# Layer 1's q and k projected as rows with the heads' rotary parts in one block, and layer 3's input transposed in the slab ahead of it

## What is computed

```python
c_q, c_kv, k_pe, z = split(x @ w_in)                  # 512, 512, 64, 2048 columns
q  = (rms_norm(c_q, q_norm) @ w_uq).reshape(B, S, 16, 128 + 64)
q_nope, q_pe = q[..., :128], apply_rope(q[..., 128:], cos, sin)
k_pe = apply_rope(k_pe[:, :, None, :], cos, sin)[:, :, 0]      # shared by all heads
kv = (rms_norm(c_kv, kv_norm) @ w_ukv).reshape(B, S, 16, 128 + 128)
k_nope, v = kv[..., :128], kv[..., 128:]
s = (q_nope . k_nope + q_pe . k_pe) * 192 ** -0.5     # causal softmax, then times v
y = o * silu(z);  x = layer_norm(x * alpha + y @ w_out)
# layer 3 begins with
proj = rmsnorm(x, norm_g) @ w_in
```

## Time and profile before

| | |
|---|---|
| median of 3 runs | 2526.69 us (2524.89 to 2526.69) |
| the profiled execution | 2524.33 us, of which span 2522.6 us |
| TensorE busy (matmuls) | 2470.3 us, 98% |
| VectorE, ScalarE busy | 1382.7 us (55%), 1233.0 us (49%) |
| the transfers' share of 16 engines | 50.3% (weights), mean 164 GB/s |
| granted TensorE clock, mean | 0.991 |

### The profile page before, as it was taken

One profiled execution on the slowest core, in us unless ns is written; L12 is line 12 of the kernel. 1 busy time (PEld: TensorE's weight loads), 2 busy tenths in 40 slices (PEclk: granted clock), 3 DMA queues, 4 the chain that ended last, 5 costly groups with the idle time before them and its releaser, 6 DMA issues.

```text
span 2522.6 us, 30023 instructions
## 1 busy us (share of the span) xinstructions
PE 2470.3 (98%) x12030; PEld 2060.6 (82%) x12030; DVE 1382.7 (55%) x1848; ACT 1233.0 (49%) x1661; POOL 125.0 (5%) x125
## 2 busy tenths in 40 slices
PE   8999999999999999989999989999999999999999
PEld 6888888888888888868888868888888887888887
DVE  5645454645464646554545565555445466746554
ACT  4454444444454445344555345555444368645443
POOL 1101010101010101000000000000000000000000
PEclk9999999999999999989999989999999999999999
DMA  7545555555555554635533545555555555433344
GB/s 239 188 159 185 166 184 167 181 164 173 171 172 175 183 167 151 217 125 187 180 117 116 186 143 177 174 184 173 182 173 164 179 184 161 137 103 117 101 134 134
DMA packets 342048, 414.49 MB, mean 164 GB/s; under 512 B 19019, under 2 KB 269093, under 8 KB 341397
## 3 DMA queue, kind: packets, MB, share of 16 engines
q1 hardware_dynamic: 340500, 405.63, 50.3%
q0 software_dynamic: 1408, 6.94, 0.7%
HBM read 410.42 MB, written 2.10 MB: 164 GB/s over the span
## 4 chain that ended last, share of the span: by engine, by line
PE 92%; DVE 3%; ACT 3%; issue 1%; SPq 0%; DMA 0%; POOL 0%; DVEq 0%; ACTq 0%
PE ps L557 26%; PE ps L559 26%; PE ps L558 26%; PE ps L972 2%; PE ps L597 2%; PE ps L712 1%; DVE wlo L1659 1%; ACT whi L1099 1%; PE ps L699 1%; PE ps L773 1%; PE ps L704 1%; PE ps L772 1%; PE ps L785 0%; PE ps L696 0%; DVE x L1758 0%
## 5 line engine op out<-in xcount | busy, mean ns | idle before, releaser
L1659 DVE TENSOR_TENSOR wlo<-raw,whi 128x1024 fp32r<-128x1024 f32 (+1 forms) x774 | 950.3, 1233 | 858.0 <-ACT whi L1099 854.8
L557 PE MATMUL ps<-whi,xh 128*128 128x512 f32 (+1 forms) x3072 | 1227.4, 400 | 6.7 <-DVE wlo L1659 6.7
L559 PE MATMUL ps<-whi,xl 128*128 128x512 f32 (+1 forms) x3072 | 1198.0, 390 | 0.0
L558 PE MATMUL ps<-wlo,xh 128*128 128x512 f32 (+1 forms) x3072 | 1195.8, 389 | 0.0
L1099 ACT CAST whi<-raw 128x1024 fp32r<-128x1024 f32 (+1 forms) x774 | 801.6, 1041 | 771.3 <-PE ps L559 766.7
L557 PEld LDWEIGHTS ps<-whi,xh 128*128 128x128 f32 x3072 | 578.6, 188 | 123.0 <-issue 12.2
L559 PEld LDWEIGHTS ps<-whi,xl 128*128 128x128 f32 x3072 | 577.6, 188 | 120.4
L558 PEld LDWEIGHTS ps<-wlo,xh 128*128 128x128 f32 x3072 | 578.9, 188 | 109.7
L1177 ACT ACTIVATE work<-work,small 128x128 f32<-128x128 f32 (+1 forms) x80 | 46.1, 577 | 155.7 <-DVE small L1769 155.7
L2387 POOL TENSOR_TENSOR work<-work 128x512 f32<-128x512 f32 x48 | 77.0, 1605 | 872.4 <-DVE work L1844 488.6
L972 PEld LDWEIGHTS ps<-work 128*128 128x128 f32 x544 | 67.7, 191 | 6.1 <-DVE work L2233 2.6
(11 more groups left out here) (366 smaller groups left out, 1319.9 us busy)
## 6 DMA issues: line engine op xcount, KB each, us to landing
raw<-in_dsa_w_in SPq DMA_DIRECT2D x320, 512.0 KB, 4.5
raw<-in_ev_w_in SPq DMA_DIRECT2D x144, 512.0 KB, 4.6
raw<-in_od_w_in SPq DMA_DIRECT2D x96, 512.0 KB, 4.5
raw<-in_mla_w_in SPq DMA_DIRECT2D x48, 512.0 KB, 4.3
raw<-in_dsa_w_out SPq DMA_DIRECT2D x32, 512.0 KB, 4.6
raw<-in_mla_w_out SPq DMA_DIRECT2D x32, 512.0 KB, 4.7
raw<-in_ev_w_out SPq DMA_DIRECT2D x32, 512.0 KB, 4.6
raw<-in_od_w_out SPq DMA_DIRECT2D x32, 512.0 KB, 4.9
```

Source lines behind the costliest of these rows:

```text
L557: pe.matmul(o, xh[:, k, tokens[tb]], hi, start=start and s + l == 0, stop=False)
L558: pe.matmul(o, xh[:, k, tokens[tb]], lo, start=False, stop=False)
L559: m = pe.matmul(o, xl[:, k, tokens[tb]], hi, start=False, stop=stop and s + l == 2)
L1659: dve.tensor_tensor(whole_half(wlo[:, h % 4], n), whole_half(raw[:, h // 2 % 4, 2 * (h % 2):2 * (h % 2) + 2], n), whole_half(whi[:, h % 4] ...
```

## The change

q and k are no longer projected with tokens on partitions and transposed afterwards. `unit_of_heads` makes the weights stationary, 128 columns at a time, and moves `xh` and `xl`: the result is q (two heads of 128), the rotary parts of the two heads in one block of 2 x 64, and k of two heads, all with features on partitions, as the scores need them. v is computed as before, 256 columns. `by_heads` loads the weights' columns in that order, by four transfers a unit instead of two. The rotation works on the block of features; its halves of 32 partitions change places, with cosine and sine tables transposed once in `norms`. The scores' rotary part contracts over all 128 rows, with a key `kpt[hh % 2]` whose other 64 rows are zero. Storage of q, k, v is double and alternates by quad; evictions are two copies per unit. The six transposing jobs, their copies and the copy of v are gone.

At layer 3's entrance, groups 0 to 5 of `turn_x(3)` are emitted in the last slab of layer 2, two behind each of its first three units, and groups 6 and 7 between the halves of `few_columns`, which writes to bank Q. ScalarE's squares come after it.

```diff
-            hq = c(TB, 4 * QH)
-            hkv = c(TB, 4 * KH)
-            v = c(TB, 4, P)
-            qt, kt, qpt = c(4, S), c(4, S), c(4, S)
-            kpt = c(S)
-            t1, t2 = c(TB, 4, 64), c(TB, 4, 64)
-            kp = c(TB, 64)
+            qt, kt = [c(4, S), c(4, S)], [c(4, S), c(4, S)]
+            qpt = [c(2, S), c(2, S)]
+            v = [c(TB, 4, P), c(TB, 4, P)]
+            kpt = [c(S), c(S)]
+            kr, cost, sint = c(S), c(S), c(S)
+            qr = c(2, S)
+            t1, t2 = c(2, S), c(2, S)
...
+        def by_heads(w, p, n):
+            places = [(e * P, e * n, P) for e in range(2)] + [(S + e * (n - P), e * n + P, n - P) for e in range(2)]
+            return 2 * n, [(lambda r, o=o, m=m: r[:, :, o:o + m],
+                            w[:, 2 * p * n + c:2 * p * n + c + m].rearrange("(t p) c -> p t c", p=P)) for o, c, m in places]
...
-                    yield by_rows(L1.wq, (2 * quad + p) * 2 * L1.QH, 2 * L1.QH, 0)
-                    yield by_rows(L1.wkv, (2 * quad + p) * 2 * L1.KH, 2 * L1.KH, 0)
+                    yield by_heads(L1.wq, 2 * quad + p, L1.QH)
+                    yield by_heads(L1.wkv, 2 * quad + p, L1.KH)
...
-                    project(nothing, N, out_bank(s), fine=fine)
+                    project(nothing, N, out_bank(s), fine=fine, then=turning_x(3) if layer == 2 and s else None)
...
+            def turning_x(layer):
+                def then(j):
+                    return (lambda: turn_x(layer, (2 * j, 2 * j + 1))) if j < 3 else None
...
+            def unit_of_heads(side, kind):
+
+                for s in range(2):
+                    h = half[0]
+                    pe.wait_ge(lo_done, h + 1)
+                    for l in range(2):
+                        k = 4 * kind + 2 * s + l
+                        first, last = s + l == 0, s + l == 2
+                        for g in range(2 if kind else 3):
+                            o = ps[:, 2 * kind + g // 2, g % 2 * S:(g % 2 + 1) * S]
+                            hi, lo = whi[:, h % 4, l, g * P:(g + 1) * P], wlo[:, h % 4, l, g * P:(g + 1) * P]
+                            pe.matmul(o, hi, xh[:, k, :], start=first and g != 1, stop=False)
+                            pe.matmul(o, lo, xh[:, k, :], start=False, stop=False)
+                            m = pe.matmul(o, hi, xl[:, k, :], start=False, stop=last and g != 0)
+                        if kind:
+                            hi, lo = whi[:, h % 4, l, S:N], wlo[:, h % 4, l, S:N]
+                            for tb in range(TB):
+                                o = ps[:, 3, tb * S:(tb + 1) * S]
+                                pe.matmul(o, xh[:, k, tokens[tb]], hi, start=first and tb == 0, stop=False)
+                                pe.matmul(o, xh[:, k, tokens[tb]], lo, start=False, stop=False)
+                                m = pe.matmul(o, xl[:, k, tokens[tb]], hi, start=False, stop=last and tb == 1)
+                        if l == 1:
+                            m.then_inc(half_done, 1)
+                        else:
+                            next(side, None)
+                    half[0] += 1
+                    next(side, None)
 
...
             def attention1(quad):
-                h0 = 16 + 4 * quad
-                yield
-                jobs = [(L1.qv, 0, P, 0), (L1.qv, 0, P, 2), (L1.kv, 0, P, 0), (L1.kv, 0, P, 2),
-                        (L1.qv, P, 64, 0), (L1.qv, P, 64, 2)]
-                pe.wait_ge(*e1_a.at(quad, "out2"))
-                pe.wait_ge(*hd_a.at(h0 - 1, "pt"))
-                pe.wait_ge(*hd_d.at(h0 - 1, "fin"))
-                for n, (src, c, m, hh0) in enumerate(jobs):
-                    if n == 2:
-                        pe.wait_ge(*e1_a.at(quad, "out3"))
-                    if n >= 3:
-                        pe.wait_ge(*p1_a.at(quad, f"copy{n - 3}"))
-                    if n == 4:
-                        pe.wait_ge(*p1_d.at(quad, "r"))
-                    for i in range(4):
-                        r = pe.transpose(ps[0:m, Q + 1 + n % 3, i * P:(i + 1) * P],
-                                         src[:, i % 2, hh0 + i // 2, c:c + m], ident[:, :])
-                    r.then_inc(*p1_p.up(f"turn{n}"))
-                    if n % 2:
-                        yield
+                h0, b = 16 + 4 * quad, quad % 2
+                yield
+                yield from turns(3)
                 for hh in range(4):
                     def scores():
                         for tb, (o, n) in enumerate(((0, P), (P, S))):
-                            pe.matmul(ps[:, Q, o:o + n], L1.qt[:, hh, tokens[tb]], L1.kt[:, hh, 0:n], start=True, stop=False)
-                            m = pe.matmul(ps[:, Q, o:o + n], L1.qpt[0:64, hh, tokens[tb]], L1.kpt[0:64, 0:n],
+                            pe.matmul(ps[:, Q, o:o + n], L1.qt[b][:, hh, tokens[tb]], L1.kt[b][:, hh, 0:n], start=True, stop=False)
+                            m = pe.matmul(ps[:, Q, o:o + n], L1.qpt[b][:, hh // 2, tokens[tb]], L1.kpt[hh % 2][:, 0:n],
                                           start=False, stop=True)
...
                     if hh == 0:
-                        pe.wait_ge(*p1_a.at(quad, "copy5"))
+                        pe.wait_ge(*e1_a.all(quad + 1))
+                        pe.wait_ge(*p1_d.at(quad, "r"))
+                        pe.wait_ge(*la_d.at(0, "k"))
                     yield from attend(h0 + hh, scores, turned, pv, 2, hh == 3)
...
-            turn_x(3)
-            few_columns(nothing, 16, 2, 3)
+            pe.wait_ge(*xt_d.at(8 * 3 + 4, "lo"))
+            few_columns(nothing, 16, Q, 3, between=lambda: turn_x(3, (6, 7)))
             side = lanes(delta_gates, delta, lru, lambda n: nothing)
-            free = [None, dg_a.at(0, "rows"), x3_a.at(0, "x"), x3_a.at(1, "x"), qk3_a.at(0, "qk"), v3_a.at(0, "v"), qk3_a.at(1, "qk"),
+            free = [add_d.at(2, "add2"), add_d.at(2, "add3"), x3_a.at(0, "x"), x3_a.at(1, "x"), qk3_a.at(0, "qk"), v3_a.at(0, "v"), qk3_a.at(1, "qk"),
                     qk3_a.at(2, "qk"), v3_a.at(1, "v"), qk3_a.at(3, "qk"), z3_d.at(0, "z"), z3_d.at(1, "z")]
...
-                jobs = [(P, L1.qt, 0), (P, L1.qt, 2), (P, L1.kt, 0), (P, L1.kt, 2), (64, L1.qpt, 0), (64, L1.qpt, 2)]
-                for n, (m, dst, hh0) in enumerate(jobs):
-                    act.wait_ge(*p1_p.at(quad, f"turn{n}"))
-                    act.copy(dst[0:m, hh0:hh0 + 2], ps[0:m, Q + 1 + n % 3, :].rearrange("p (h t) -> p h t", h=2)) \
-                        .then_inc(*p1_a.up(f"copy{n}"))
-                    if n == 1:
-                        act.wait_ge(*hd_p.at(h0 - 1, "pv"))
-                        act.wait_ge(*e1_a.all(quad + 1))
-                        act.copy(L1.v, L1.kv[:, :, :, P:]).then_inc(*p1_a.up("v"))
-                    if n % 2:
-                        yield
+                yield from turns(3)
...
-                            if quad:
-                                act.wait_ge(*p1_p.at(quad - 1, ("turn5", "turn3")[kind]))
-                            act.copy(dst[:, :, p * n:(p + 1) * n], ps[:, 2 * kind:2 * kind + 2, 0:n]) \
-                                .then_inc(*e1_a.up(f"out{2 * p + kind}"))
+                            b = quad % 2
+                            if quad >= 2:
+                                act.wait_ge(*hd_p.at(16 + 4 * quad - 5, "pv"))
+                            if kind == 0:
+                                act.copy(L1.qt[b][:, 2 * p:2 * p + 2, :], ps[:, 0, :].rearrange("p (h t) -> p h t", h=2))
+                                if quad:
+                                    act.wait_ge(*p1_d.at(quad - 1, "r"))
+                                m = act.copy(L1.qr[:, p, :], ps[:, 1, 0:S])
+                            else:
+                                act.copy(L1.kt[b][:, 2 * p:2 * p + 2, :], ps[:, 2, :].rearrange("p (h t) -> p h t", h=2))
+                                m = act.copy(L1.v[b][:, :, 2 * p:2 * p + 2, :],
+                                             ps[:, 3, :].rearrange("p (t h c) -> p t h c", t=TB, h=2))
+                            m.then_inc(*e1_a.up(f"out{2 * p + kind}"))
                         unit(side, then=evict)
...
-            turn_x(3)
-            side = squares(3)
-            few_columns(side)
-            run(side)
+            few_columns(nothing, lambda: turn_x(3, (6, 7)))
             act.wait_ge(half_done, half[0])
-            act.copy(L3.rdec[0:16], ps[0:16, 2, 0:S]).then_inc(*dg_a.up("rows"))
+            act.copy(L3.rdec[0:16], ps[0:16, Q, 0:S]).then_inc(*dg_a.up("rows"))
+            run(squares(3))
             side = lanes(delta_gates, delta, lru, lambda n: nothing)
...
-                cb, sn = bc(cosb[:, :, :], 2, 4), bc(sinb[:, :, :], 2, 4)
                 dve.wait_ge(*e1_a.at(quad, "out2"))
                 dve.wait_ge(*(p1_d.at(quad - 1, "r") if quad else la_d.at(0, "k")))
-                dve.tensor_tensor(L1.t1, L1.qr, cb, ALU.mult)
```

(9 more changed lines are left out.)

128 lines of the change are left out of this document (73 added, 55 removed).

## The result

The changed kernel takes **2508.27 us** (median of 4 runs, 2507.24 to 2509.25), the kernel before in the same rounds 2525.79 (2523.27 to 2526.69): ratio **0.9932, 95% interval 0.9915 to 0.9949**. The profiled execution took 2509.25 us, its span 2507.5.

What follows compares the result with a forecast made beforehand. TensorE, busy 98% of 2522.6 us, was taken as the bound. Terms -12.0 - 0.1 + 2.1 - 1.4 = -11.4 us, from the median 2526.69, gave 2515.3 us; own range 2511 to 2519.5, wider range 2509.5 to 2522.5.

Steps and rivals of the forecast that it cites:

- part 2: Layer 1's quads: dropping 24 transposes each takes 12.0 us off TensorE; ScalarE's fewer copies and the padded scores count nothing.
- the scores' term: Layer 1's score matmuls: same moving columns, 64 padded rows cost none, so zero change.
- rival 1: Layer 1's 256-column matmuls need over 0.113 us as loads show; fully unhidden 2565 us; chance 0.08 large, 0.08 partial.
- The transposes: Layer 1: three blocks of eight gone per quad, 3 x 3.07 + 2.76 = 12.0 us off TensorE's chain.
- The products: Layer 1's q, k, v up-projections as 256-column matmuls: same columns, zero change; bounds 0.7 us gain, 50 us loss.
- the load shows: Rival 1: loading 128 stationary columns lengthens a 256-column matmul's spacing; chance 0.08 beyond 17 ns plus noise, 0.08 partly.
- a part of it, 5 to 10 ns: Small form of rival 1: 5 to 10 ns more per layer-1 product matmul, 2519 to 2522 us; chance 0.08.
- The late link: Layer 1: first scores wait 0.7 us for VectorE's 3.85 us rotation in three quads, not the fourth; 2.1 us on.
- Layer 3's entrance: Layer 2's last slab to layer 3's first wide product: 10.77 us becomes 9.4, 1.4 us off; bounds 0 and 2.0.
- The transfers: Layer 1's weights: packets per quad rise from 2048 to 8192, time goes by bytes, zero cost, hidden behind four buffers.
- the 32-partition products: Rival on VectorE's rotation: products crossing partitions cost twice, waits of 3.1 us in three quads, 2522.5 us; chance 0.07.
- evictions or casts: Rival: transposes were cover, ScalarE's evictions or casts end last without them, the gain halves to 2521 us; chance 0.05.

Runs made afterwards that it cites:

- turns_back: Kernel after with 24 unused 128x128 transposes put back at each layer-1 quad's end, ahead of the first scores: 2519.56 us, ratio 0.9965 to the kernel before.

## Why the prediction was wrong

**The step that failed** is the last sentence of part 2: "The scores keep their columns; 64 padded rows cost none, since a matmul's time goes by its moving columns." It put the scores' term at nothing. The columns are the same and the time isn't: 12.5 us went there, more than the transposes gave. The rule was taken from matmuls whose stationary operands all had the same rows. The scores' matmuls alternate between 128 and 64, and their starts were in the trace: 1.99 us a head, where the starts of the kernel after's equal-row matmuls give 1.12. The prediction had read the rows up to the first of them and not gone on; its rival 1 says that "all rows here use all row groups", which holds for the rows that it lists and not for the scores' rotary part. With 16 x 0.78 its sum would have been -23.9, a forecast of 2502.8, 5.5 too low: the missing term was larger than the miss of 6.1 us in the gain, because the products (3.3) and the waits not foreseen (2.4) stood on the other side. That the forecast came as near as it did is in part luck.

**The transposes** (-12.0) were right: 11.6 by the blocks of the kernel before, 10.6 for the same number put back by hand. The 1.0 between them is waiting, most of it for ScalarE's copies, which the prediction had counted as a dearer third block. That blocks of transposes are paid whole held also for the fourth quad.

**The products** (0, with 0.7 us of gain as one bound) went the other way, +3.3. The rival "the load shows" had exactly this mechanism with "a part of it, 5 to 10 ns"; measured are 6.6 ns a matmul over 0.1133. The row taken as nearest, products with v at 0.112 us, was of another type and of 128 moving columns, and did not carry over; 0.120 is above the 0.118 that the prediction named as its limit. The trace had a sign against "0.443 ns per column" as well: the prediction gives 0.170 us for 384 columns, and they stand 0.175 apart on average, and never closer than 0.171 away from the blocks. So the narrower product was already the dearer one per column. As to the Trainium skill, "TensorE: Matmul & The Clock Gate", section "What overlaps and what doesn't": that loads overlap only where row groups differ is not what these traces show. A load of 191 ns hides, but for 7 ns, behind starts 120 ns apart with the same rows on both sides, and the loads that don't hide are those at a change of rows.

**The late link** (+2.1) was right in place and size: 2.5, the rotation 4.2 us and not 3.85. What it missed is the fourth quad, where it held the scores to be safe ("6.8 us behind"). They are, but by 0.15 us: the rotation's sum ends at 1367.68 and the scores start at 1367.83. And what VectorE has queued behind the rotation is late. Timelines of VectorE and TensorE in the output product of the kernel after:

```profile
1366.99 0.69 DVE L1965 TENSOR_TENSOR work<-work 128x512 f32<-128x512 f32 x1
1367.60 1.22 DVE L1692 TENSOR_TENSOR wlo<-raw,whi 128x1024 fp32r<-128x1024 f32 x1
...
1368.74 1.28 DVE L1741 TENSOR_TENSOR xl<-ps,xh 128x512 fp32r<-128x512 f32 x2
...
1369.94 1.21 DVE L1692 TENSOR_TENSOR wlo<-raw,whi 128x1024 fp32r<-128x1024 f32 x1
1371.07 0.28 DVE L1807 CUSTOM_DVE_ANT_0 work<-ps,work 128x128 f32<-128x128 f32 x1
...
1372.98 0.44 PE L806 MATMUL ps<-ident,work 128*128 128x128 f32 x2 [0.92 <-ACT work L1213]
```

The scores were issued from 1367.83 on and read at 1371.07, behind two splits and the low half of y; the exponentials came late by 1.1 us. The prediction had asked what is queued behind the rotation, and had checked only the weights.

**Layer 3's entrance** (-1.4) was right, 1.31 in two kernels. **The transfers** (0) were right in what they cost TensorE, though a kilobyte took 56 ns and not 49 beside the quads. Of the rivals, the 32-partition products cost 0.69 us each, not twice as much, and no evictions or casts ended last.

## What to carry to other kernels

Before costing a matmul by its columns, look whether its neighbours' stationary operands have the same rows: each change between 64 and 128 rows cost 0.20 us here. Padding with zeros to 128 rows removed it at no price on TensorE; putting the short ones next to each other removed half. In an engine's stream the cheap place for a movable piece of work is right behind something another engine waits for, not right ahead of it, and an engine with 44% of its time idle can still be late at every such place. A change that takes cover away shows waits far from where the work was, so a sum needs what is queued behind the moved work, in every stage that it is queued in.

## What the runs showed of the hardware that was not expected

- At a change of the stationary operand's row count the load isn't made ahead: 0.20 us each (four, two and none of them in a head: 2.11, 1.73 and 1.33 us). The moving operand's rows change with it; the two were not tried apart.
- The width of the stationary operand shows in the spacing of fp32r matmuls: 0.1199 us with 128 columns and 0.1134 with 64, both moving 256.
- VectorE's products of 32 partitions x 512 elements last as long (0.69 us) as those of 128 partitions, also when they write to other partitions than they read.
- Up to 5 us of a whole execution are decided by TensorE's clock at one place of layer 3 that the change doesn't touch. There TensorE waits 1.36 us for ScalarE and then issues sixteen matmuls of one column. The same lines in the kernel after and in the kernel with the rotation cut in two:

```profile
2142.22 1.95 PE L1016 MATMUL ps<-ones,work 128*128 128x1 f32 x16 [1.36 <-ACT work L1594]
2144.34 0.39 PE L567 MATMUL ps<-wlo,xh 128*128 128x512 f32 x1
...
2157.81 0.38 PE L1031 MATMUL ps<-work 128*128 128x128 f32 x2
```

```profile
2141.14 2.76 PE L1016 MATMUL ps<-ones,work 128*128 128x1 f32 x16 [1.36 <-ACT work L1594]
...
2144.34 0.63 PE L567 MATMUL ps<-wlo,xh 128*128 128x512 f32 x1
...
2161.88 0.38 PE L1031 MATMUL ps<-work 128*128 128x128 f32 x2
```

From the first to the last row it is 15.6 us in one and 20.7 in the other. In the second the granted clock is 0.60 and 0.71 in the stretches 2140 to 2150 and 2150 to 2160 us, that is 1.2 GHz for most of it (a 512-column matmul every 0.43 us instead of 0.227), where the first has 1.00. The low clock at this place lasts 13.7 us in this execution and in the profiled one of `turns_back`, the two with a mean of 0.988, and none, 3.4 or 6.8 us in the others. In the kernel before, 6 of 15 executions of one chip show a mean clock of 0.989 and take 2529.5 to 2530.7 us, the rest 2523.3 to 2527.6; that theirs is the same place was not profiled.
